# The rotary turn of q and k: a matmul with a permutation matrix replaced by four 32-partition transfers and a new column order

## What is computed

```python
def apply_rope(x, cos, sin):
    b, s, h, _ = x.shape
    xs = x.astype(jnp.float32).reshape(b, s, h, 2, 2, ROPE_FREQS)   # (axis, half, 16 frequencies)
    rot = jnp.stack([-xs[..., 1, :], xs[..., 0, :]], axis=-2)
    return (xs * cos + rot * sin).reshape(b, s, h, HEAD_DIM).astype(x.dtype)
...
        hx = modulate(rms_norm(x, g_mix[l]), sh1, sc1)
        hc = modulate(rms_norm(ctx, g_mix[l]), csh1, csc1)
        px = split_cols(hx @ w_in[l], IN_SIZES)
        q = apply_rope(px[0].reshape(b, s, N_HEADS, HEAD_DIM), cos, sin)
        k = apply_rope(px[1].reshape(b, s, N_KV_HEADS, HEAD_DIM), cos, sin)
...
        y_attn = windowed_latent_attention(q, k, v, kc, vc, sink)
```

## Time and profile before

| | us |
|---|---|
| median of 3 runs | 1287.19 |
| lowest and highest | 1286.8, 1289.53 |
| the profiled execution, its own time | 1287.43 |
| its span in the trace | 1285.6 |
| TensorE busy | 1258.6 (98%) |
| VectorE busy | 879.0 (68%) |
| ScalarE busy | 554.2 (43%) |

### The profile page before, as it was taken

One profiled execution on the slowest core, in us unless ns is written; L12 is line 12 of the kernel. 1 busy time (PEld: TensorE's weight loads), 2 busy tenths in 40 slices (PEclk: granted clock), 3 DMA queues, 4 the chain that ended last, 5 costly groups with the idle time before them and its releaser, 6 DMA issues.

```text
span 1285.6 us, 19927 instructions
## 1 busy us (share of the span) xinstructions
PE 1258.6 (98%) x7682; PEld 1090.3 (85%) x7682; DVE 879.0 (68%) x1184; ACT 554.2 (43%) x874; POOL 301.7 (23%) x254
## 2 busy tenths in 40 slices
PE   5999999999999999999999999999999999999998
PEld 3788777777788898888888888898889998999998
DVE  4696888753699677663779774485787567765664
ACT  4322355644333245332223332244576545653553
POOL 0005299310142101111001110002693130220222
PEclk9999999999999999999999999999999999999999
DMA  9464511222356435653545664334433553564561
GB/s 368 169 219 163 176 62 62 74 66 67 119 185 237 129 101 167 194 192 124 176 148 191 211 198 147 105 115 144 164 120 101 182 178 132 187 218 153 180 218 43
DMA packets 49762, 198.75 MB, mean 155 GB/s; under 512 B 5520, under 2 KB 5904, under 8 KB 48528
## 3 DMA queue, kind: packets, MB, share of 16 engines
q1 hardware_dynamic: 49680, 197.62, 46.7%
HBM read 196.55 MB, written 1.05 MB: 154 GB/s over the span
## 4 chain that ended last, share of the span: by engine, by line
PE 90%; DVE 6%; ACT 2%; issue 1%; DMA 1%; SPq 0%; DVEq 0%; ACTq 0%
PE psA L533 26%; PE psA L535 25%; PE psA L534 25%; PE psB L533 2%; PE psB L535 2%; PE psB L534 2%; DVE w_lo L1327 2%; PE psB L809 1%; PE psB L821 1%; DVE acc L1593 1%; PE psA L793 1%; PE psB L736 1%; PE psB L554 1%; DVE small L1606 1%; ACT w_hi L1008 1%
## 5 line engine op out<-in xcount | busy, mean ns | idle before, releaser
L533 PE MATMUL psA<-h_hi,w_hi 128*128 128x256 f32 (+1 forms) x1528 | 520.0, 340 | 3.7 <-DVE h_lo L1475 2.6
L534 PE MATMUL psA<-h_lo,w_hi 128*128 128x256 f32 (+1 forms) x1528 | 512.9, 336 | 0.0
L535 PE MATMUL psA<-h_hi,w_lo 128*128 128x256 f32 (+1 forms) x1528 | 512.9, 336 | 0.0
L1327 DVE TENSOR_TENSOR w_lo<-raw,w_hi 128x1024 fp32r<-128x1024 f32 (+2 forms) x244 | 336.2, 1378 | 90.5 <-ACT w_hi L1008 90.4
L1008 ACT ACTIVATE w_hi<-raw 128x1024 fp32r<-128x1024 f32 (+2 forms) x244 | 276.9, 1138 | 280.8 <-PE psA L535 208.7
L533 PEld LDWEIGHTS psA<-h_hi,w_hi 128*128 128x128 f32 x1528 | 291.1, 190 | 37.7 <-issue 4.9
L535 PEld LDWEIGHTS psA<-h_hi,w_lo 128*128 128x128 f32 x1528 | 291.2, 191 | 29.6
L534 PEld LDWEIGHTS psA<-h_lo,w_hi 128*128 128x128 f32 x1528 | 291.4, 191 | 28.7 <-issue 0.2
L518 POOL TENSOR_TENSOR hid_lo<-sig,hid_hi 128x512 f32 (+3 forms) x44 | 67.3, 1529 | 471.5 <-ACT hid_hi L1287 471.5
L1348 DVE SCALAR_TENSOR_TENSOR ada_sum<-raw,csil,ada_sum 128x1024 f32<-128x1024 f32 x112 | 154.6, 1411 | 0.0
L533 PE MATMUL psA<-hid_hi,w_hi 128*128 128x256 f32 (+1 forms) x352 | 116.0, 330 | 0.0
(11 more groups left out here) (204 smaller groups left out, 1493.8 us busy)
## 6 DMA issues: line engine op xcount, KB each, us to landing
raw<-w_up SPq DMA_DIRECT2D x88, 512.0 KB, 4.2
raw<-w_ada SPq DMA_DIRECT2D x80, 512.0 KB, 3.6
raw<-w_dn SPq DMA_DIRECT2D x32, 704.0 KB, 5.1
raw<-w_in SPq DMA_DIRECT2D x36, 512.0 KB, 4.3
raw<-w_at SPq DMA_DIRECT2D x24, 512.0 KB, 3.5
raw<-w_fn SPq DMA_DIRECT2D x16, 640.0 KB, 4.5
raw<-w_sc SPq DMA_DIRECT2D x16, 640.0 KB, 3.8
raw<-w_cf SPq DMA_DIRECT2D x16, 640.0 KB, 4.0
```

Source lines behind the costliest of these rows:

```text
L533: pe.matmul(out, w0, hi, start=first, stop=False)
L534: pe.matmul(out, w0, lo, start=False, stop=False)
L535: return pe.matmul(out, w1, hi, start=False, stop=last)
L1327: dve.tensor_tensor(w_lo[:, s, 0:tiles * P], raw[:, r, 0:tiles * P], w_hi[:, s, 0:tiles * P].bitcast(F32), ALU.subtract).then_inc(rest_don ...
```

## The change

The columns of w_in for q and k are put in another order within each head: (axis, half, frequency) becomes (half, axis, frequency), so that partners lie 32 partitions apart. The cos and sin tables follow, and sin carries the sign. The matrix `rot` and the five matmuls per layer are gone, with TensorE's waits on them and VectorE's on the result. In their place ScalarE issues four DMAs for each tile, each of 32 partitions x 256 columns (32 KB), SBUF to SBUF, which write the tile with neighbouring quarters crossed into `swap[j]` (halves of `sig[0]` and `sig[1]`, and `sqa` for k). `SWAP_AT = {2: 0, 3: 1, 4: 2, 5: 3, 13: 4}` says where; ScalarE waits there for the copy of the tile. VectorE's three operations stay, the first now in place on `swap[j]`, behind a wait for the landing. In layer 0 they stay behind chunks 5 to 8 and 14, in layer 1 those of q move to chunks 8 to 11. `fourier_channels` waits for `evac` n0+8 instead of the turn.

```diff
-ROT_AT = {5: 0, 6: 1, 7: 2, 8: 3, 14: 4}
+ROPE_AT = [{5: 0, 6: 1, 7: 2, 8: 3, 14: 4}, {8: 0, 9: 1, 10: 2, 11: 3, 14: 4}]
+SWAP_AT = {2: 0, 3: 1, 4: 2, 5: 3, 13: 4}
...
+        swap = [sig[j // 2][:, SEQ * (j % 2):SEQ * (j % 2 + 1)] for j in range(4)] + [sqa[:, 0:SEQ]]
...
                 def fourier_channels():
 
-                    pe.wait_ge(rope, 15 * layer + 12)
-                    pe.wait_ge(evac, n0 + 6)
+                    if layer == 0:
+                        pe.wait_ge(mats_late, 16)
+                    pe.wait_ge(evac, n0 + 8)
...
-                    if idx in ROT_AT:
-
-                        j = ROT_AT[idx]
-                        if layer == 0 and j == 0:
-                            pe.wait_ge(mats_late, 16)
-                        pe.wait_ge(evac, n0 + (j if j < 4 else 12) + 1)
-                        if j >= 2:
-                            pe.wait_ge(rope, 15 * layer + 3 * (j - 2) + 1)
-                        if j == 4:
-                            pe.wait_ge(fn_rest, fc0 + 2 * streams(layer))
-                        src = q[:, j, 0:SEQ] if j < 4 else k_all[:, 0:SEQ]
-                        pe.matmul(psB[1 + 2 * (j % 2)][:, 0:SEQ], M("rot"), src, start=True, stop=True)\
-                            .then_inc(rot, 1)
...
+            def swap_halves(n0, j):
+
+                act.wait_ge(evac, n0 + (j if j < 4 else 12) + 1)
+                src = q[:, j, 0:SEQ] if j < 4 else k_all[:, 0:SEQ]
+                for quarter in range(4):
+                    act.dma_start(swap[j][32 * quarter:32 * quarter + 32, :],
+                                  src[32 * (quarter ^ 1):32 * (quarter ^ 1) + 32, :]).then_inc(swapped[j], 16)
...
                     if layer and idx < KD:
                         shifted_head(layer, 0, 1, idx)
+                    if idx in SWAP_AT:
+                        swap_halves(n0, SWAP_AT[idx])
...
-                        dve.wait_ge(rot, 5 * layer + j + 1)
-                        if j >= 2:
-                            dve.wait_ge(rope, r - 3)
-                        dve.tensor_tensor(tmp[j % 2][:, 0:SEQ], psB[1 + 2 * (j % 2)][:, 0:SEQ], M("sin", SEQ),
-                                          ALU.mult).then_inc(rope, 1)
+                        if layer == 0 and j == 0:
+                            dve.wait_ge(mats_late, 16)
+                        dve.wait_ge(swapped[j], 64 * (layer + 1))
+                        dve.tensor_tensor(swap[j], swap[j], M("sin", SEQ), ALU.mult).then_inc(rope, 1)
                         dve.tensor_tensor(dst, dst, M("cos", SEQ), ALU.mult).then_inc(rope, 1)
                         dve.wait_ge(rope, r + 2)
-                        dve.tensor_tensor(dst, dst, tmp[j % 2][:, 0:SEQ], ALU.add).then_inc(rope, 1)
+                        dve.tensor_tensor(dst, dst, swap[j], ALU.add).then_inc(rope, 1)
...
-        wq = tiles(w[:, heads])
+        wq = tiles(w[:, heads].reshape(D, N_HEADS, 2, 2, HEAD // 4).swapaxes(2, 3).reshape(D, -1))
+        wk = tiles(w[:, Q_W:Q_W + KV_W].reshape(D, KV_W // HEAD, 2, 2, HEAD // 4).swapaxes(2, 3).reshape(D, -1))
```

More of the change, by code:

```diff
@@ L112 @@
 MAT, _at = {}, 0
-for _name, _n in [("ident", 128), ("mean", 128), ("fold", 32), ("rot", 128), ("chan", 256), ("pos", 1024),
+for _name, _n in [("ident", 128), ("mean", 128), ("fold", 32), ("chan", 256), ("pos", 1024),
                   ("cos", 256), ("sin", 256)]:
@@ L296, in program @@
             "sq_done", "sq_sum", "stat", "root", "inv", "ht", "h_head", "h_rest"))
-        pads, rot, rope, fc_mm, fc, fn_mm, fn_head, fn_rest = map(sem, (
-            "pads", "rot", "rope", "fc_mm", "fc", "fn_mm", "fn_head", "fn_rest"))
+        swapped = [sem(f"swapped{j}") for j in range(5)]
+        pads, rope, fc_mm, fc, fn_mm, fn_head, fn_rest = map(sem, (
+            "pads", "rope", "fc_mm", "fc", "fn_mm", "fn_head", "fn_rest"))
         sc_step, sc_head, sc_rest, sigd = map(sem, ("sc_step", "sc_head", "sc_rest", "sigd"))
@@ L396, in _ @@
                 sp.dma_start(X[:, 2 * j:2 * j + 2, :], io["x"][:, 2 * j:2 * j + 2, :]).then_inc(x_full[j], 16)
-            sp.dma_start(mat[:, 0:MAT["rot"]], io["mat"][:, 0:MAT["rot"]]).then_inc(mats_in, 16)
+            sp.dma_start(mat[:, 0:MAT["chan"]], io["mat"][:, 0:MAT["chan"]]).then_inc(mats_in, 16)
             for c in range(KD):
@@ L405, in _ @@
                     .then_inc(first_in[c], 16)
-            sp.dma_start(mat[:, MAT["rot"]:NMAT], io["mat"][:, MAT["rot"]:NMAT]).then_inc(mats_late, 16)
+            sp.dma_start(mat[:, MAT["chan"]:NMAT], io["mat"][:, MAT["chan"]:NMAT]).then_inc(mats_late, 16)
             sp.dma_start(acc[:, 0, 0:2 * P], io["band"]).then_inc(band_in, 16)
@@ L1567, in _ @@
                         dve.tensor_copy(v[:, :, :].rearrange("p b n -> p (b n)"), psB[2][:, :]).then_inc(v_done, 1)
-                    if idx in ROT_AT:
-                        j = ROT_AT[idx]
+                    if idx in ROPE_AT[layer]:
+                        j = ROPE_AT[layer][idx]
                         dst = q[:, j, 0:SEQ] if j < 4 else k_all[:, 0:SEQ]
                         r = 15 * layer + 3 * j
-                        dve.wait_ge(rot, 5 * layer + j + 1)
-                        if j >= 2:
-                            dve.wait_ge(rope, r - 3)
-                        dve.tensor_tensor(tmp[j % 2][:, 0:SEQ], psB[1 + 2 * (j % 2)][:, 0:SEQ], M("sin", SEQ),
-                                          ALU.mult).then_inc(rope, 1)
+                        if layer == 0 and j == 0:
+                            dve.wait_ge(mats_late, 16)
+                        dve.wait_ge(swapped[j], 64 * (layer + 1))
+                        dve.tensor_tensor(swap[j], swap[j], M("sin", SEQ), ALU.mult).then_inc(rope, 1)
                         dve.tensor_tensor(dst, dst, M("cos", SEQ), ALU.mult).then_inc(rope, 1)
                         dve.wait_ge(rope, r + 2)
-                        dve.tensor_tensor(dst, dst, tmp[j % 2][:, 0:SEQ], ALU.add).then_inc(rope, 1)
+                        dve.tensor_tensor(dst, dst, swap[j], ALU.add).then_inc(rope, 1)
                     if layer == 0:
@@ L1818, in constants @@
     put("fold", np.tile(np.eye(32), (4, 1)))
[L1820 to L1826, removed]
     c = np.arange(64)
@@ L1843, in constants @@
         for half in range(2):
-            a[axis * 32 + half * 16:axis * 32 + half * 16 + 16] = pos[axis][None, :] * inv[:, None]
+            a[half * 32 + axis * 16:half * 32 + axis * 16 + 16] = pos[axis][None, :] * inv[:, None]
     m[:, MAT["cos"]:MAT["cos"] + SEQ] = np.tile(np.cos(a), (2, 1))
-    m[:, MAT["sin"]:MAT["sin"] + SEQ] = np.tile(np.sin(a), (2, 1))
+    side = np.where(np.arange(P) % 64 < 32, -1.0, 1.0)[:, None].astype(np.float32)
+    m[:, MAT["sin"]:MAT["sin"] + SEQ] = np.tile(np.sin(a), (2, 1)) * side
     return m
```

## The result

The changed kernel takes 1291.86 us (median of 15 runs, 1289.36 to 1295.02), the kernel before beside it 1287.19 us (15 runs). The ratio is 1.0037, 95% interval 1.0029 to 1.0044: slower by 0.37%. The forecast was 1286.3 us and no change; the time lies above the range. The profiled execution of after took 1290.87 us, its span 1289.1.

What follows compares the result with a forecast made beforehand. TensorE's matmul starts were taken to bound the kernel. From the profiled 1287.43 us, -2.25 - 3.88 + 4d with d = 1.3 gave 1286.5, or 1286.3 us as a median; forecast's own range 1285.5 to 1288.9, 8-in-10 range 1281.0 to 1289.2.

Steps and rivals of the forecast that it cites:

- What bounds the kernel: Whole kernel: TensorE, busy 98% of the span; when matmuls start counts, and time between two is paid in full.
- Part 1: Layer 0: five fp32 turn matmuls gone, 0.45 us each with nothing in their shadow, gaining 2.25 us.
- Part 2: Layer 1 without ScalarE's new issues: Fourier product 3.45 us earlier, limited by `w_lo`; with k's 0.43, 3.88 us.
- Part 3: Layer 1's loop: sixteen DMA issues on ScalarE, four per round at chunks 2 to 5, delay the Fourier product by 4d.
- d: Delay four issues add to one round of layer 1's loop, between h block and `w_hi`; taken as 1.3 us.
- the issues cost more than SyncE's in a row: Layer 1, h block to `w_hi`, chunks 2 to 5: d 2.2 to 2.8, 1289.9 to 1292.3 us; chance 0.13.
- The sum: Whole kernel: -2.25 - 3.88 + 4d against the profiled 1287.43 us; in general 1281.1 + 4d.
- Part 4: Layer 0's issues, landings, swap traffic and VectorE's operations cost nothing; late k bound 0 to 1 us on VectorE, 0 at end.
- The first rival: Layer 1's issues on ScalarE nearly free, d of 0 to 0.4, 1281.1 to 1282.7 us; chance 0.20.
- The third rival: Layer 0's saved TensorE time is lost at a later wait, only layer 1 changes: 1288.6 us; chance 0.05.

Runs made afterwards that it cites:

- the kernel with only this part: Against the kernel before: layer 0 turns by transfers, layer 1 keeps TensorE's turn with the new column order; 1283.06 us, ratio 0.9974.

## Why the prediction was wrong

**What bounds the kernel** was right: the time followed TensorE's starts, stretch by stretch.

**Part 1** (2.25 us in layer 0) held: 2.31 by the trace, and the kernel with only this part has ratio 0.9974, 3.3 us, with 2.25 inside its interval (1.9 to 4.8 us).

**Part 2** (3.45 us to the Fourier product, 0.43 for k) held: 3.36 without issues on ScalarE, and `w_lo` at 3.14 us as worked out. k's turn: from layer 1's Fourier stage to attention the table loads of ScalarE stand 9.91 us apart before (897.51, 907.42) and 9.49 after (900.24, 909.73), 0.42. Its assumption that VectorE's operations are worth moving was tested apart, 1.15 us.

**Part 3** failed, in one step: "I take 1.3, because four equal issues in a row are what the two rows of 1.8 us show". The place, the overlap with the h block, the chain through `w_hi`, `w_lo` and scaled, and "the Fourier product moves by the whole 4d" all held. The size was that of other transfers. SyncE's rows are transfers of 128 rows with one end in DRAM. With a DRAM source the pieces gave d = 1.46, the upper end I had named (1.45), and waits of 0.93, 1.46, 1.45 and 1.45 us where the forecast's own d would have given 0.8 and 1.6. With the source in SBUF four issues take 2.44 us, d = 2.13. So the rows were near in number and not in the one property that mattered, both ends in SBUF, and no row of before has a transfer from SBUF to SBUF on a hardware queue. I gave the end above 0.46 per issue a rival with 0.13, when nothing in the trace spoke of such transfers. That rival ("the issues cost more than SyncE's in a row", d from 2.2) is nearly what happened.

**The clock** was missing: two stretches at half clock, behind waits of 2.16 and 2.26 us that I had forecast at 1.6, of which the second cost 1.3 us. Waits were priced by their length alone, although before's trace has a fall behind waits of 0.55, 0.55 and 1.80 us.

The sum, from the median of before: 1281.1 + 4 x 2.13 + 1.3 = 1290.9 us, 0.9 under the measured 1291.86. From the profiled execution of before (1287.43 - 6.13 = 1281.3) it gives 1291.1, against 1290.87 of the profiled execution of after. That this meets so closely is partly luck: a start that was 1.54 us shorter and a stretch near 1090 us that was 1.1 longer, with the half clock there, than in before's profile nearly cancel.

**Part 4** held. VectorE waited for no landing; q's and k's land in 1.8 to 5.3 us. In layer 0 the issues hide in ScalarE's wait for loads.

**The first rival** (issues nearly free) is refuted for this place and right six chunks further: behind the h blocks the same sixteen issues cost nothing in the stretch. The Trainium skill, page "DMA: Bandwidth & Descriptors", section "Issuing engines are not separate DMA queues", calls the time to initiate a DMA usually small relative to the DMA itself. Here it is 0.61 us to a median of 3.0 to landing, and the comparison doesn't help: what counts is what stands behind the issue. The Trainium skill, page "Perfetto Trace Analysis", section "DMA Instruction — HWDGE (DVE, Sync)", says that the profiled time of such an instruction is that in which its sequencer is held, up to its release. The rows agree: `w_hi` starts at 854.24, 0.10 us behind the end of four issues at 854.14.

**The third rival** (saving lost elsewhere) didn't happen: from layer 0's last turn to layer 1, the landmarks are 677.09 us apart before (147.10, 824.19) and 677.21 after (143.25, 820.46).

## What to carry to other kernels

A DMA issue is an instruction of its engine, with a price by the piece: put it where that engine has slack or where nothing that others wait for stands behind it. Inside a loop through several engines every round pays it again: here four rounds of 2.13 us. Price a transfer by a row with the same kind of source and target and the same place in a row of issues; if there is none, keep both ends and give the far one a real chance, or cut the pieces to one. Look in the trace of before for windows at half clock and the waits ahead of them; when a forecast wait nears those, it can cost more than its length. The version in which SyncE issues is 0.4 to 0.6% under the kernel before and differs from the changed one only in who issues sixteen DMAs; the one with ScalarE's issues behind the h blocks has the same stretch and can't be told from it by the times.

## What was not expected of the hardware

- A transfer from SBUF to SBUF takes 0.61 us to issue in a row on ScalarE and 0.59 on SyncE, alone 0.47 to 0.53; a piece of the same shape from DRAM 0.44 in a row, four stores from SBUF to DRAM 0.44, and SyncE's single loads of 512 KB 0.33. Rows and bytes hardly matter: 128 rows in one transfer took 0.49.
- The first issue starts 0.01 us behind the activation ahead of it and runs beside it.
- Single issues of the same form took up to 2.19 us without another issue beside them.
- In this stretch the granted clock fell to half behind waits of 2.16 us and more, and not behind waits of 1.56 us or less, four of 0.93 to 1.46 us included. Near 1086 us it fell in every profile, before's too, behind waits of 0.55, 0.55 and 1.80 us. So no single length of wait tells it.
